# A low pass that contracts 64 rows, and one shared buffer for the low parts of two query sets

## The chip, the cores and the metric

The kernel runs on one core of one Trainium2 chip. The metric is the device time of one execution in microseconds (us); the time of a kernel is the median of its runs. The core's engines are named as the profile names them: PE is TensorE's matmul, PEld its weight load, DVE is VectorE, ACT is ScalarE, POOL is GpSimd and SP is SyncE, which issues most transfers.

## The reference

One decoder layer over 2048 tokens of width 1024, all in float32. An input projection feeds two head groups. Group A, which the change touches, is sparse attention with 8 query heads of 64 over 2 shared key heads. An indexer scores every key for every query, the 256 best causal keys are kept, and softmax attention runs over them:

```python
rel = jax.nn.relu(jnp.einsum('bthd,bsd->btsh', qib, ki))      # index scores, 8 heads x 64
iscore = jnp.einsum('btsh,bth->bts', rel, wib)
_, idx = lax.top_k(iscore, topk)                              # topk = 256
s = jnp.einsum('btgrd,btkgd->btgrk', qg, ksel) * (HEAD_DIM ** -0.5)
p = jax.nn.softmax(s, axis=-1)
o = jnp.einsum('btgrk,btkgd->btgrd', p, vsel)
```

Group B is a gated linear recurrence (HGRN2). Both groups' outputs pass an output projection, a norm and a residual, then a SwiGLU layer of width 2816 with its own norms and residual.

## The kernel before

The program has two phases. The first (`project_hgrn_phase`, up to some 890 us) makes the input projection and the recurrence. The second, `mixer_phase`, has the attention of 16 blocks of 128 queries, and lays the output projection and the SwiGLU layer between the attention's steps: `fills` gives each attention step ("slot") its share of these items by a table of weights, so that PE always has dense matmuls between two attention steps. All engines walk through the same slots, each in its own fixed order, and meet by semaphores.

Matmuls use the type fp32r, which keeps only a high part of a float32. So each operand is split: the high part is a copy that rounds, the low part is what remains. The dense products take three matmuls (high by high, high by low, low by high). The attention has head dimension 64, half of PE's 128 rows, and uses the other half for the split of the keys. The tile `KT` holds for each of three key sets (two key heads, one index key set, number `KV`) the high part on partitions 0 to 63 and the low part on 64 to 127. The queries `qT` and the index queries `qiT` have two planes: plane 0 has the high part of the queries on both halves of the partitions, plane 1 the low part on both halves. `two_passes` then needs two matmuls of 128 rows for queries by keys: plane 0 by `KT` is high by (high and low), plane 1 by `KT` is low by (high and low).

Per block the pieces of this are made as follows. `open_split` (PE, L1980) transposes 64 columns of the projected rows into the PSUM tile `SA`, eight times for queries, three times for keys. `high` (ACT) copies out the high part: keys in one instruction of 64x384 (L1524), queries in two of 64x1024, one for each half of the partitions (L1528, L1529). `low` (DVE) subtracts high from `SA` and gives the low part: keys straight to partitions 64 to 127 (L1696), queries to partitions 0 to 63 of plane 1 (L1704). `double` (ACT, L1538) copies that plane to partitions 64 to 127 and tells PE by the semaphores `q_doubled` and `qi_doubled`. `openings` says when: the queries of block b+1 at the last head of block b, the index queries and keys of block b+2 one head earlier. That makes 16 sets of queries and 14 of index queries, which blocks 0 and 1 don't need.

PE waits for `doubled` twice per block: before the index scores of block b+1 (`idx`) and before the scores of block b (`scores`). The index scores are read by ACT (L1546) and summed by DVE (L1716); the scores are read by DVE (L1810), go through the exponential on ACT (L1562), are transposed by PE (L2011), copied by ACT (L1574) and multiplied with the values by PE (L2025). `SA` has two halves that all of these take in turn.

Of the kernel before, what the change touches and what calls it, by code (L numbers as in the profile page):

```python
# [29 lines left out]
HEADS, KV, HD = 8, 2, 64  # L30
GROUP = HEADS // KV
ATT = HEADS * HD
IH = 8
# [16 lines left out]
SM_SCALE = HD ** -0.5  # L50
# [795 lines left out]
def mixer_phase(nc, a, proj_d, mix_d, x1_d, out, kept):  # L846
# [28 lines left out]
    for s in range(NS):  # L875
# [12 lines left out]
        for g, (f0, f1) in enumerate(GROUPS):  # L888
            last = f1 - 1 if g == NG - 1 else f1
# [95 lines left out]

    for b in range(NB):
        for c in range(pairs_of(b + 1) if 2 <= b + 1 < NB else 0):
            w = min(1024, NK(b + 1) - 1024 * c) / 1024
# [14 lines left out]
    for s in range(-1, NS - 1):  # L1003
# [3 lines left out]
        last = at["out", s + 1, 0, 0, 0] - 1  # L1007
        if s < 0:
            window = window[PARTS_FROM:]
            last = FIRST - 1  # L1010
# [13 lines left out]
    with ExitStack() as ctx:  # L1024
        def sb(name, shape, dt=F32):
            return ctx.enter_context(nc.sbuf_tensor(name, shape, dt))
# [10 lines left out]
        def sem(name):  # L1037
            return ctx.enter_context(nc.semaphore("m_" + name))
# [2 lines left out]
        wis = sb("wis", [P, 2, IH])  # L1041
        KT, acc_last = sb_two("KT", [P, 3, T], "acc_last", [P, 6, D])
        V = sb("V", [P, NB, KV * HD])
        qT = sb("qT", [P, 2, HEADS, P], F32R)
        qiT = sb("qiT", [P, 2, IH, P], F32R)
        score = sb("score", [P, T + 8])
        bias = sb("bias", [P, 2, T], BF16)
        ends = sb("ends", [P, 2])
# [45 lines left out]
        iota_ready = sem("iota_ready")  # L1094
        rows_ready, value0_ready = sem("rows_ready"), sem("value0_ready")
        hi_out = sem("hi_out")
        doubled = {"q": sem("q_doubled"), "qi": sem("qi_doubled")}
        sa_full = sem("sa_full")
        sa_free_act, sa_free_dve, pt_ready = sem("sa_free_act"), sem("sa_free_dve"), sem("pt_ready")
        rel_read = sem("rel_read")  # L1100
# [27 lines left out]
        use, reader, pt_order, idx_order, hi_order = {}, [], {}, {}, {}  # L1128
# [46 lines left out]
        def pair(key):  # L1175
            return SA[:, use[key] % 2, :]
# [3 lines left out]
        for key in use:  # L1180
            who = reader[use[key]]
            if who == "pt":
                _, b, h, p = key
# [7 lines left out]
        def wait_pair_read(eng, n):  # L1191
            eng.wait_ge(*pair_read[n])
# [5 lines left out]
        def wait_pair_full(eng, key):  # L1198
            eng.wait_ge(sa_full, use[key] + 1)
# [42 lines left out]
        def heads(ap, n):  # L1242
            return ap.rearrange("p (h t) -> p h t", h=n)
# [272 lines left out]
        def _(act):  # L1516
            s_ = nc.scalar

            def high(key):

                what, b = key
                wait_pair_full(act, key)
                if what == "keys":
                    s_.activation(KT[0:HD, :, b * P:(b + 1) * P], heads(pair(key)[0:HD, 0:3 * P], 3), ACT.Copy)\  # L1524
                      .then_inc(hi_out, 1)
                else:
                    to, scale = (qT, -SM_SCALE) if what == "q" else (qiT, 1.0)
                    s_.activation(to[HD:P, 0], heads(pair(key)[0:HD], 8), ACT.Copy, scale=scale)  # L1528
                    s_.activation(to[0:HD, 0], heads(pair(key)[0:HD], 8), ACT.Copy, scale=scale)\  # L1529
                      .then_inc(hi_out, 1)  # L1530

            def double(b, h):

                for key in openings(b, h):
                    if key[0] != "keys":
                        to = qT if key[0] == "q" else qiT
                        wait_pair_read(act, use[key])
                        s_.activation(to[HD:P, 1], to[0:HD, 1].bitcast(F32), ACT.Copy).then_inc(doubled[key[0]], 1)  # L1538

            def idx(b, c, h):  # L1540
                w = min(1024, NK(b) - 1024 * c)
# [106 lines left out]

            for key in openings(-1, 0):
                high(key)  # L1650
            double(-1, 0)
            for b in range(NB):
                for c in range(pairs_of(b + 1) if 2 <= b + 1 < NB else 0):
                    for h in range(IH):
                        idx(b + 1, c, h)
                        fill(("i", b, c, h))
                softmax(b, 0)
                fill(("s", b))
                for h in range(HEADS):
                    for key in openings(b, h):  # L1660
                        high(key)
                        if key[0] == "qi":
                            fill(("O", b, 0))
                    fill(("A", b, h))
                    turned_probs(b, h, 0)
                    fill(("B", b, h))
                    if h + 1 < HEADS:
                        softmax(b, h + 1)
                    if pairs_of(b) == 2:
                        turned_probs(b, h, 1)  # L1670
                        fill(("C", b, h))
                    for k in search(b, h, "B"):
                        count(b + 1, k)
                    double(b, h)
            for n in range(TAIL[0], LAST_STEP):
                step(n)

# [2 lines left out]
        def _(dve):  # L1680
            v = nc.vector
# [8 lines left out]
            def low(key):  # L1690

                what, b = key
                dve.wait_ge(hi_out, hi_order[key] + 1)
                if what == "keys":
                    cols = slice(b * P, (b + 1) * P)
                    v.tensor_tensor(KT[HD:P, :, cols], heads(pair(key)[0:HD, 0:3 * P], 3),  # L1696
                                    KT[0:HD, :, cols].bitcast(F32), ALU.subtract).then_inc(sa_free_dve, 1)
                else:
                    to = (qT if what == "q" else qiT)[0:HD]
                    if what == "q" and b >= 1:  # L1700
                        dve.wait_ge(doubled["q"], b)
                    if what == "qi" and b >= 3:
                        dve.wait_ge(doubled["qi"], b - 2)
                    v.scalar_tensor_tensor(to[:, 1], heads(pair(key)[0:HD], 8), -SM_SCALE if what == "q" else 1.0,  # L1704
                                           to[:, 0].bitcast(F32), ALU.mult, ALU.subtract).then_inc(sa_free_dve, 1)

            def accumulate(b, c, h):
                w = min(1024, NK(b) - 1024 * c)
# [253 lines left out]
        def _(pe):  # L1962
            t = nc.tensor
# [16 lines left out]
                    last = t.transpose(pair(key)[0:HD, h * P:(h + 1) * P], row[:, b % 2, c0:c0 + HD], ident[:])  # L1980
                last.then_inc(sa_full, 1)

            def two_passes(to, q, k):
                t.matmul(to, q[:, 0], k, start=True, stop=False)  # L1984
                return t.matmul(to, q[:, 1], k, start=False, stop=True)  # L1985

            def idx(b, c, h):
                key = ("idx", b, c, h)
                take(key)
                for k0 in range(1024 * c, min(NK(b), 1024 * (c + 1)), 512):  # L1990
                    w = min(512, NK(b) - k0)
                    last = two_passes(pair(key)[:, k0 - 1024 * c:k0 - 1024 * c + w], qiT[:, :, h, :], KT[:, KV, k0:k0 + w])
                last.then_inc(sa_full, 1)

            def scores(b, h):
                for p in range(pairs_of(b)):
                    key = ("att", b, h, p)
                    take(key)
                    for k0 in range(1024 * p, min(NK(b), 1024 * (p + 1)), 512):
                        w = min(512, NK(b) - k0)  # L2000
                        last = two_passes(pair(key)[:, k0 - 1024 * p:k0 - 1024 * p + w], qT[:, :, h, :],
                                          KT[:, h // GROUP, k0:k0 + w])
                    last.then_inc(sa_full, 1)

            def turn_probs(b, h, p):
# [99 lines left out]
            for b in range(NB):  # L2105
                if 2 <= b + 1 < NB:
                    wait_pair_read(pe, use["keys", b + 1])
                    pe.wait_ge(doubled["qi"], b)
                    for c in range(pairs_of(b + 1)):
                        for h in range(IH):  # L2110
                            idx(b + 1, c, h)
                            fill(("i", b, c, h))
                wait_pair_read(pe, use["keys", b])
                pe.wait_ge(doubled["q"], b + 1)
                scores(b, 0)
                fill(("s", b))
                for h in range(HEADS):
                    if h + 1 < HEADS:
                        scores(b, h + 1)
                    for key in openings(b, h):  # L2120
                        open_split(key)
                        if key[0] == "qi":
                            fill(("O", b, 0))
                    fill(("A", b, h))
                    for p in range(pairs_of(b)):
                        turn_probs(b, h, p)
                        fill(("BC"[p], b, h))
                        values(b, h, p)
# [51 lines left out]
```

## Time and profile before

| | us |
|---|---|
| median of 3 runs | 3378.53 |
| lowest, highest run | 3377.57, 3380.3 |
| the profiled execution | 3383.49 |
| its span, first to last instruction | 3381.5 |

| engine | busy us | share |
|---|---|---|
| PE | 3214.6 | 95% |
| PEld | 2836.7 | 84% |
| DVE | 2267.9 | 67% |
| ACT | 1501.5 | 44% |
| POOL | 237.1 | 7% |

Starts and durations in the rows are from one profiled execution. A row of the timeline gives the start, the duration, the engine and line, the tiles written and read, and in brackets how long the engine was idle before it and what ended that. Matmuls are pipelined: the next one starts before the end of the last, so the distance from start to start is what one costs, not its duration. The last column of a waiting engine's row names what came last by the profile.

### The profile page before, as it was taken

How to read it: one execution, taken by the hardware profiler on the slowest of the kernel's cores; microseconds unless marked ns; L12 is line 12 of the kernel's file. 1: busy time of each engine (PE TensorE's matmuls, PEld its weight loads, DVE VectorE, ACT ScalarE, POOL GpSimd, SP SyncE). 2: the span in 40 equal slices, each digit the busy share in tenths (PEclk: the TensorE clock that was granted, in tenths of full speed). 3: DMA queues.
4: the chain of work that ended last, by engine and by line, in shares of the span. 5: the costliest groups of instructions: out<-in, count | busy, mean ns of one | idle time of the engine just before them, and what ended most of it. 6: DMA issues, size and time to landing. Idle time of an engine off the chain costs nothing.

```text
span 3381.5 us, 46512 instructions
## 1 busy us (share of the span) xinstructions
PE 3214.6 (95%) x18048; PEld 2836.7 (84%) x18048; DVE 2267.9 (67%) x3817; ACT 1501.5 (44%) x2477; POOL 237.1 (7%) x400
## 2 busy tenths in 40 slices
PE   8999999999888899999989999998999999989998
PEld 8999999998777788888778888887888888868886
DVE  3467777788565766666787777677876765463445
ACT  3454455445455454443554444445554444333222
POOL 0000000000111110010110001011000000010000
PEclk9999999999899999999989999999999999999999
DMA  5543443344222222222522212134111112252233
GB/s 182 168 134 121 131 149 125 114 139 130 98 84 104 94 83 80 68 85 69 180 83 76 71 63 79 64 111 150 63 65 60 64 52 74 95 182 97 91 105 107
DMA packets 147501, 345.66 MB, mean 102 GB/s; under 512 B 15057, under 2 KB 35921, under 8 KB 145233
## 3 DMA queue, kind: packets, MB, share of 16 engines
q1 hardware_dynamic: 144976, 338.49, 30.2%
q10 hardware_dynamic: 2304, 4.20, 0.3%
q8 instruction: 144, 2.36, 0.3%
q14 instruction: 77, 0.62, 0.1%
HBM read 283.31 MB, written 59.31 MB: 101 GB/s over the span
## 4 chain that ended last, share of the span: by engine, by line
PE 63%; DVE 5%; ACT 2%; issue 2%; DMA 1%; SPq 0%; DVEq 0%; POOL 0%; ACTq 0%; POOLq 0%
PE PJ_d L2069 9%; PE PJ_d L2071 9%; PE PJ_d L2070 9%; PE SC L2025 7%; PE PJ_d L2094 6%; PE PJ_d L2096 6%; PE PJ_d L2095 6%; PE SA L1984 3%; PE SA L2011 3%; PE SA L1985 3%; PE SA L1980 1%; DVE score L1716 1%; DVE wd_lo L1825 1%; DVE prob L1810 1%; DVE h_lo L1830 0%
## 5 line engine op out<-in xcount | busy, mean ns | idle before, releaser
L2069 PE MATMUL PJ_d<-h_hi,wd_hi 128*128 128x512 f32 (+1 forms) x1472 | 577.1, 392 | 15.4 <-DVE h_lo L1830 9.9
L2071 PE MATMUL PJ_d<-h_hi,wd_lo 128*128 128x512 f32 (+1 forms) x1472 | 564.6, 384 | 0.0
L2070 PE MATMUL PJ_d<-h_lo,wd_hi 128*128 128x512 f32 (+1 forms) x1472 | 563.8, 383 | 0.0
L1579 ACT ACTIVATE wd_hi<-wd_raw 128x512 fp32r<-128x512 f32 x568 | 345.2, 627 | 229.6 <-DMA wd_raw<-in_w_gu 128.6
L733 PE MATMUL PJ<-w_hi,h_hi 128*128 128x338 f32 (+1 forms) x1280 | 416.0, 325 | 2.8 <-DVE w_lo L550 2.8
L1825 DVE TENSOR_TENSOR wd_lo<-wd_raw,wd_hi 128x512 fp32r<-128x512 f32 x568 | 380.5, 689 | 45.9 <-ACT wd_hi L1579 42.9
L734 PE MATMUL PJ<-w_lo,h_hi 128*128 128x338 f32 (+1 forms) x1280 | 408.6, 319 | 0.0
L735 PE MATMUL PJ<-w_hi,h_lo 128*128 128x338 f32 (+1 forms) x1280 | 408.5, 319 | 0.0
L1574 ACT ACTIVATE pT<-SA 128x512 f32<-128x512 f32 (+3 forms) x320 | 156.6, 532 | 519.4 <-PE SA L2011 519.4
L1810 DVE CUSTOM_DVE_ANT_0 prob<-SA,bias 128x1024 f32<-128x1024 f32 (+7 forms) x192 | 170.1, 911 | 314.2 <-PE SA L1985 306.9
L2069 PEld LDWEIGHTS PJ_d<-h_hi,wd_hi 128*128 128x128 f32 x1472 | 280.8, 191 | 66.4 <-DVE wd_lo L1825 6.8
L2071 PEld LDWEIGHTS PJ_d<-h_hi,wd_lo 128*128 128x128 f32 x1472 | 280.4, 190 | 54.8
L2070 PEld LDWEIGHTS PJ_d<-h_lo,wd_hi 128*128 128x128 f32 x1472 | 281.2, 191 | 48.7
L2025 PEld LDWEIGHTS SC<-V,pT 128*128 128x128 f32 x2176 | 273.9, 194 | 38.1 <-ACT pT L1574 26.6
L2025 PE MATMUL SC<-V,pT 128*128 128x64 f32 x2176 | 271.1, 274 | 19.8 <-ACT pT L1574 19.8
L2094 PE MATMUL PJ_d<-wd_hi,hid 128*128 128x512 f32 x704 | 282.0, 401 | 6.9 <-DVE acc L1864 3.6
L2096 PE MATMUL PJ_d<-wd_hi,hid 128*128 128x512 f32 x704 | 276.1, 392 | 0.0
L2095 PE MATMUL PJ_d<-wd_lo,hid 128*128 128x512 f32 x704 | 275.6, 391 | 0.0
L428 ACT ACTIVATE stage<-PJ 128x338 f32<-128x338 f32 (+1 forms) x160 | 72.7, 454 | 430.6 <-PE PJ L735 430.6
L733 PEld LDWEIGHTS PJ<-w_hi,h_hi 128*128 128x128 f32 x1280 | 242.5, 189 | 5.4 <-issue 3.1
L734 PEld LDWEIGHTS PJ<-w_lo,h_hi 128*128 128x128 f32 x1280 | 243.0, 190 | 2.3
L735 PEld LDWEIGHTS PJ<-w_hi,h_lo 128*128 128x128 f32 x1280 | 242.1, 189 | 0.0
(207 smaller groups left out, 5724.6 us busy)
## 6 DMA issues: line engine op xcount, KB each, us to landing
wd_raw<-in_w_gu SPq DMA_DIRECT2D x352, 256.0 KB, 2.9
wd_raw<-in_w_down SPq DMA_DIRECT2D x176, 256.0 KB, 2.6
w_raw<-in_w_in SPq DMA_DIRECT2D x40, 684.0 KB, 4.6
w_raw<-in_w_in SPq DMA_DIRECT2D x40, 676.0 KB, 4.5
row_h<-proj_d SPq DMA_DIRECT2D x16, 1024.0 KB, 7.0
proj_d<-stage SPq DMA_DIRECT2D x40, 342.0 KB, 4.5
proj_d<-stage SPq DMA_DIRECT2D x40, 338.0 KB, 5.0
x_d<-acc SPq DMA_DIRECT2D x24, 512.0 KB, 2.9
```

Source lines behind the costliest of these rows:

```text
L733: t.matmul(out, h_hi[:, k, tok], w_hi[:, u, e], start=(k == 0), stop=False)
L734: t.matmul(out, h_hi[:, k, tok], w_lo[:, u, e], start=False, stop=False)
L735: last = t.matmul(out, h_lo[:, k, tok], w_hi[:, u, e], start=False, stop=(k == KD - 1))
L1579: s_.activation(w_hi[:, u % RING, :], w_raw[:, u % RING, :], ACT.Copy).then_inc(w_hi_ready, 1)
L1825: v.tensor_tensor(w_lo[:, u % RING, :], w_raw[:, u % RING, :], w_hi[:, u % RING, :].bitcast(F32), ALU.subtract).then_inc(w_lo_ready, 1)
L2025: last = t.matmul(SC[:, h * HD:(h + 1) * HD], pT[:, m % 2, (kb % 4) * P:(kb % 4 + 1) * P], V[:, kb, g * HD:(g + 1) * HD], start=(kb == 0), ...
L2069: t.matmul(to[:, tok], w_hi[:, r, w], h_hi[:, c, tok], start=(c == 0 and part != 1), stop=False)
L2070: t.matmul(to[:, tok], w_hi[:, r, w], h_lo[:, c, tok], start=False, stop=False)
L2071: last = t.matmul(to[:, tok], w_lo[:, r, w], h_hi[:, c, tok], start=False, stop=(c == KD - 1 and part != 0))
L2094: t.matmul(to, hi, w_hi[:, r, :], start=(k == parts[0]), stop=False)
L2095: t.matmul(to, hi, w_lo[:, r, :], start=False, stop=False)
L2096: last = t.matmul(to, lo, w_hi[:, r, :], start=False, stop=(k == parts[-1]))
```

## The change

The high parts stay as they were, on both halves of the partitions, but `qT` and `qiT` lose their second plane. A new tile `qlow` holds both low parts: that of the queries on partitions 0 to 63, that of the index queries on 64 to 127. The second matmul of `two_passes` contracts only the 64 rows on which the low part lies, with the high part of the keys. For the index keys that needs the high part on partitions 64 to 127, so the index set of `KT` is stored with its halves exchanged, and the copy and the subtraction of the keys become two instructions each on ACT and DVE. `double` and its semaphores go; PE waits for DVE's low part itself. The product of the low part of the queries with the low part of the keys is no longer in the sum.

```diff
-        qT = sb("qT", [P, 2, HEADS, P], F32R)
-        qiT = sb("qiT", [P, 2, IH, P], F32R)
+        qT = sb("qT", [P, HEADS, P], F32R)
+        qiT = sb("qiT", [P, IH, P], F32R)
+        qlow = sb("qlow", [P, HEADS, P], F32R)
...
                 if what == "keys":
-                    s_.activation(KT[0:HD, :, b * P:(b + 1) * P], heads(pair(key)[0:HD, 0:3 * P], 3), ACT.Copy)\
-                      .then_inc(hi_out, 1)
+                    cols = slice(b * P, (b + 1) * P)
+                    s_.activation(KT[0:HD, 0:KV, cols], heads(pair(key)[0:HD, 0:KV * P], KV), ACT.Copy)
+                    s_.activation(KT[HD:P, KV, cols], pair(key)[0:HD, KV * P:(KV + 1) * P], ACT.Copy).then_inc(hi_out, 1)
...
-            def double(b, h):
-
-                for key in openings(b, h):
-                    if key[0] != "keys":
-                        to = qT if key[0] == "q" else qiT
-                        wait_pair_read(act, use[key])
-                        s_.activation(to[HD:P, 1], to[0:HD, 1].bitcast(F32), ACT.Copy).then_inc(doubled[key[0]], 1)
...
                 if what == "keys":
                     cols = slice(b * P, (b + 1) * P)
-                    v.tensor_tensor(KT[HD:P, :, cols], heads(pair(key)[0:HD, 0:3 * P], 3),
-                                    KT[0:HD, :, cols].bitcast(F32), ALU.subtract).then_inc(sa_free_dve, 1)
+                    v.tensor_tensor(KT[HD:P, 0:KV, cols], heads(pair(key)[0:HD, 0:KV * P], KV),
+                                    KT[0:HD, 0:KV, cols].bitcast(F32), ALU.subtract)
+                    v.tensor_tensor(KT[0:HD, KV, cols], pair(key)[0:HD, KV * P:(KV + 1) * P],
+                                    KT[HD:P, KV, cols].bitcast(F32), ALU.subtract).then_inc(sa_free_dve, 1)
+                elif what == "q":
+                    v.scalar_tensor_tensor(qlow[0:HD], heads(pair(key)[0:HD], 8), -SM_SCALE, qT[0:HD].bitcast(F32),
+                                           ALU.mult, ALU.subtract).then_inc(sa_free_dve, 1)
                 else:
...
+                    v.tensor_tensor(qlow[HD:P], heads(pair(key)[0:HD], 8), qiT[HD:P].bitcast(F32),
+                                    ALU.subtract).then_inc(sa_free_dve, 1)
...
-            def two_passes(to, q, k):
-                t.matmul(to, q[:, 0], k, start=True, stop=False)
-                return t.matmul(to, q[:, 1], k, start=False, stop=True)
+            def two_passes(to, high, k, low, k_high):
+                t.matmul(to, high, k, start=True, stop=False)
+                return t.matmul(to, low, k_high, start=False, stop=True)
...
-                    last = two_passes(pair(key)[:, k0 - 1024 * c:k0 - 1024 * c + w], qiT[:, :, h, :], KT[:, KV, k0:k0 + w])
+                    last = two_passes(pair(key)[:, k0 - 1024 * c:k0 - 1024 * c + w], qiT[:, h, :], KT[:, KV, k0:k0 + w],
+                                      qlow[HD:P, h, :], KT[HD:P, KV, k0:k0 + w])
...
-                        last = two_passes(pair(key)[:, k0 - 1024 * p:k0 - 1024 * p + w], qT[:, :, h, :],
-                                          KT[:, h // GROUP, k0:k0 + w])
+                        last = two_passes(pair(key)[:, k0 - 1024 * p:k0 - 1024 * p + w], qT[:, h, :],
+                                          KT[:, h // GROUP, k0:k0 + w], qlow[0:HD, h, :], KT[0:HD, h // GROUP, k0:k0 + w])
...
-                    pe.wait_ge(doubled["qi"], b)
+                    wait_pair_read(pe, use["qi", b + 1])
...
-                pe.wait_ge(doubled["q"], b + 1)
+                wait_pair_read(pe, use["q", b])
```

On ACT, around the end of block 0's attention, this stood in a row before: the openings of index queries (L1528, L1529), keys (L1524) and queries, each set of queries followed by its copy (L1538), and then the index scores of block 2 (L1546).

```order
534 L1529 ACTIVATE qiT<-SA 64x1024
535 L1606 ACTIVATE acc<-PJ_d 128x512
536 L1579 ACTIVATE wd_hi<-wd_raw_9646 128x512
537 L1524 ACTIVATE KT<-SA 64x3x128
538 L1574 ACTIVATE pT<-SA 128x128
539 L1562 ACTIVATE prob,den<-prob,nmx 128x128
540 L1538 ACTIVATE qiT<-qiT 64x1024
541 L1528 ACTIVATE qT<-SA 64x1024
542 L1529 ACTIVATE qT<-SA 64x1024
543 L1606 ACTIVATE acc<-PJ_d 128x512
544 L1574 ACTIVATE pT<-SA 128x128
545 L1538 ACTIVATE qT<-qT 64x1024
546 L1546 ACTIVATE prob<-SA 128x384 x3
```

In the changed kernel, with its own line numbers (the keys are L1525 and L1526, the queries L1529 and L1530, the index scores L1539), the same place reads:

```order
535 L1530 ACTIVATE qiT<-SA 64x1024
536 L1599 ACTIVATE acc<-PJ_d 128x512
537 L1572 ACTIVATE wd_hi<-wd_raw_9646 128x512
538 L1525 ACTIVATE KT<-SA 64x2x128
539 L1526 ACTIVATE KT<-SA 64x128
540 L1567 ACTIVATE pT<-SA 128x128
541 L1555 ACTIVATE prob,den<-prob,nmx 128x128
542 L1529 ACTIVATE qT<-SA 64x1024
543 L1530 ACTIVATE qT<-SA 64x1024
544 L1599 ACTIVATE acc<-PJ_d 128x512
545 L1567 ACTIVATE pT<-SA 128x128
546 L1539 ACTIVATE prob<-SA 128x384 x3
```

Both copies are gone, the keys have two instructions, and nothing else has moved. On PE, at the start of the second phase (11 transposes, then the scores of the first two heads), the rows before were:

```order
4390 L1980 MATMUL SA<-ident,xt 64x128 x11
4391 L1984 MATMUL SA<-KT,qT 128x128
4392 L1985 MATMUL SA<-KT,qT 128x128
4393 L1984 MATMUL SA<-KT,qT 128x128
4394 L1985 MATMUL SA<-KT,qT 128x128
4395 L2036 MATMUL PJ_d<-ident,tile_9647 128x128 x4
```

and now they are:

```order
4390 L1971 MATMUL SA<-ident,xt 64x128 x11
4391 L1975 MATMUL SA<-KT,qT 128x128
4392 L1976 MATMUL SA<-KT,qlow 128x128
4393 L1975 MATMUL SA<-KT,qT 128x128
4394 L1976 MATMUL SA<-KT,qlow 128x128
4395 L2028 MATMUL PJ_d<-ident,tile_9647 128x128 x4
```

PE has as many matmuls in the same order, with as many columns; every second one of a pair now reads 64 rows of `qlow` and `KT`.

## Rows read from the trace of the kernel before

**Rows 1.** The page: busy time, share of the span, instructions of each engine.

```profile
PE 3214.6 (95%) x18048; PEld 2836.7 (84%) x18048; DVE 2267.9 (67%) x3817; ACT 1501.5 (44%) x2477; POOL 237.1 (7%) x400
```

**Rows 2.** Stages: stretch, length; busy of PE, PEld, DVE, ACT, POOL; granted clock; DMA share.

```profile
890.00:1110.00 220.00, 184.37 (x958) 150.14 (x958) 124.65 (x338) 119.04 (x241) 38.14 (x90) 0.92 0.29 104
...
2600.00:2940.00 340.00, 336.81 (x1868) 290.20 (x1867) 210.75 (x341) 141.85 (x220) 4.48 (x2) 1.00 0.22 73
```

**Rows 3.** Line 1985, the low pass: count, min/median/max ns, first and last start.

```profile
L1985 PE MATMUL SA<-KT,qT x320: 272/390/628, 898.8 to 2932.9; 128*128 128x512 f32 x136, 128*128 128x128 f32 x8, 128*128 128x256 f32 x8, 128*128 128x384 f32 x8
...
L1985 PE MATMUL SA<-KT,qiT x304: 272/390/628, 931.9 to 2665.0; 128*128 128x512 f32 x136, 128*128 128x384 f32 x8, 128*128 128x128 f32 x4, 128*128 128x256 f32 x4
```

**Rows 4.** Timeline of PE: values of one head, then scores of the next.

```profile
2043.80 0.78 PE L2025 MATMUL SC<-V,pT 128*128 128x64 f32 x6
2044.39 0.48 PE L1984 MATMUL SA<-KT,qT 128*128 128x512 f32 x1
2044.70 0.39 PE L1985 MATMUL SA<-KT,qT 128*128 128x512 f32 x1
2044.93 0.40 PE L1984 MATMUL SA<-KT,qT 128*128 128x512 f32 x1
2045.16 0.40 PE L1985 MATMUL SA<-KT,qT 128*128 128x512 f32 x1
```

**Rows 5.** Timeline of PE: three transposes with a tile of 128*64 between dense matmuls.

```profile
1185.94 0.39 PE L2071 MATMUL PJ_d<-h_hi,wd_lo 128*128 128x512 f32 x1
1186.17 0.49 PE L1980 MATMUL SA<-ident,xt 128*64 128x128 f32 x3
1186.42 0.48 PE L2069 MATMUL PJ_d<-h_hi,wd_hi 128*128 128x512 f32 x1
1186.73 0.39 PE L2070 MATMUL PJ_d<-h_lo,wd_hi 128*128 128x512 f32 x1
```

**Rows 6.** Timeline of PE: three transposes with the full tile, then dense matmuls.

```profile
2040.71 0.50 PE L2011 MATMUL SA<-ident,prob 128*128 128x128 f32 x3
2040.96 0.48 PE L2094 MATMUL PJ_d<-wd_hi,hid 128*128 128x512 f32 x1
2041.28 0.39 PE L2095 MATMUL PJ_d<-wd_lo,hid 128*128 128x512 f32 x1
```

**Rows 7.** Timeline of all engines at the start of the second phase.

```profile
896.10 1.22 DVE L1704 SCALAR_TENSOR_TENSOR qT<-SA,qT 64x1024 fp32r<-64x1024 f32 x1 [1.81 <-ACT qT L1529]
...
897.35 1.05 ACT L1538 ACTIVATE qT<-qT 64x1024 fp32r<-64x1024 f32 x1 [1.28 <-DVE qT L1704]
...
898.51 0.45 PE L1984 MATMUL SA<-KT,qT 128*128 128x128 f32 x1 [4.52 <-ACT qT L1538]
...
901.01 1.11 PE L2036 MATMUL PJ_d<-ident,tile 128*128 128x128 f32 x4 [1.42 <-DMA tile<-mix_d]
```

**Rows 8.** Waits of PE from 914 to 1110 us: total us, times, longest.

```profile
PE SC L2025 <- ACT pT L1574: 10.6, 17, 2.0
...
PE SA L1984 <- ACT prob L1546: 4.1, 9, 1.9
```

**Rows 9.** Timeline at the end of block 0: the copy, the index scores, PE.

```profile
931.50 1.06 ACT L1538 ACTIVATE qT<-qT 64x1024 fp32r<-64x1024 f32 x1 [0.19 <-DVE qT L1704]
...
932.58 0.87 ACT L1546 ACTIVATE prob<-SA 128x384 f32<-128x384 f32 x2
...
933.12 0.44 PE L1984 MATMUL SA<-KT,qiT 128*128 128x384 f32 x1 [0.57 <-ACT prob L1546]
```

**Rows 10.** Timeline at a late copy: what PE has meanwhile.

```profile
1467.55 1.67 PE L2025 MATMUL SC<-V,pT 128*128 128x64 f32 x14
```

**Rows 11.** By line: the copy, the keys on ACT, the keys on DVE (min/median/max ns).

```profile
L1538 ACT ACTIVATE qT<-qT x16: 1054/1058/1064, 897.4 to 2810.1; 64x1024 fp32r<-64x1024 f32 x16
...
L1524 ACT ACTIVATE KT<-SA x16: 471/485/488, 893.2 to 2592.5; 64x384 fp32r<-64x384 f32 x16
...
L1696 DVE TENSOR_TENSOR KT<-SA,KT x16: 550/551/552, 893.7 to 2593.4; 64x384 fp32r<-64x384 f32 x16
```

More of the change, by code:

```diff
@@ L1096, in mixer_phase @@
         hi_out = sem("hi_out")
-        doubled = {"q": sem("q_doubled"), "qi": sem("qi_doubled")}
         sa_full = sem("sa_full")
@@ L1523, in high @@
                 if what == "keys":
-                    s_.activation(KT[0:HD, :, b * P:(b + 1) * P], heads(pair(key)[0:HD, 0:3 * P], 3), ACT.Copy)\
-                      .then_inc(hi_out, 1)
+                    cols = slice(b * P, (b + 1) * P)
+                    s_.activation(KT[0:HD, 0:KV, cols], heads(pair(key)[0:HD, 0:KV * P], KV), ACT.Copy)
+                    s_.activation(KT[HD:P, KV, cols], pair(key)[0:HD, KV * P:(KV + 1) * P], ACT.Copy).then_inc(hi_out, 1)
                 else:
                     to, scale = (qT, -SM_SCALE) if what == "q" else (qiT, 1.0)
-                    s_.activation(to[HD:P, 0], heads(pair(key)[0:HD], 8), ACT.Copy, scale=scale)
-                    s_.activation(to[0:HD, 0], heads(pair(key)[0:HD], 8), ACT.Copy, scale=scale)\
+                    s_.activation(to[HD:P], heads(pair(key)[0:HD], 8), ACT.Copy, scale=scale)
+                    s_.activation(to[0:HD], heads(pair(key)[0:HD], 8), ACT.Copy, scale=scale)\
                       .then_inc(hi_out, 1)
-            def double(b, h):
-                for key in openings(b, h):
-                    if key[0] != "keys":
-                        to = qT if key[0] == "q" else qiT
-                        wait_pair_read(act, use[key])
-                        s_.activation(to[HD:P, 1], to[0:HD, 1].bitcast(F32), ACT.Copy).then_inc(doubled[key[0]], 1)
             def idx(b, c, h):
@@ L1650, in _ @@
                 high(key)
-            double(-1, 0)
             for b in range(NB):
@@ L1673, in _ @@
                         count(b + 1, k)
-                    double(b, h)
             for n in range(TAIL[0], LAST_STEP):
@@ L1695, in low @@
                     cols = slice(b * P, (b + 1) * P)
-                    v.tensor_tensor(KT[HD:P, :, cols], heads(pair(key)[0:HD, 0:3 * P], 3),
-                                    KT[0:HD, :, cols].bitcast(F32), ALU.subtract).then_inc(sa_free_dve, 1)
-                else:
[L1699 to L1705, printed above, removed]
+                    v.tensor_tensor(KT[HD:P, 0:KV, cols], heads(pair(key)[0:HD, 0:KV * P], KV),
[5 more added lines that the diff above has]
+                                           ALU.mult, ALU.subtract).then_inc(sa_free_dve, 1)
+                else:
+                    v.tensor_tensor(qlow[HD:P], heads(pair(key)[0:HD], 8), qiT[HD:P].bitcast(F32),
+                                    ALU.subtract).then_inc(sa_free_dve, 1)
             def accumulate(b, c, h):
```

## The prediction

> **What bounds the kernel now.** I read the busy times first: PE is busy for 95% of the span, ACT for 44%, DVE for 67% [rows 1]. Then the stages: in the stretch in which the second phase starts PE is idle for 220 - 184.4 = 35.6 us, in a late one with long rows of keys for only 340 - 336.8 = 3.2 us [rows 2]. So from about the third block on the end of the kernel is set by the number of matmuls and by their distance from start to start, and only the first 220 us of the phase have idle time that lighter work on another engine could give back. Third, the passes that the change touches: the low pass runs 320 times for scores and 304 times for index scores, 624 in all, up to 512 columns each, and most of the phase long [rows 3]. From start to start one such matmul takes 0.23 us (2044.70 to 2044.93 to 2045.16), while its duration reads 0.39 to 0.40 [rows 4]: each starts 0.16 to 0.17 us before the end of the last. The dense matmuls have the same distance.
>
> **Part 1, the copy on ACT goes.** It is 16 copies of queries and 14 of index queries, 1.06 us each [rows 11], 31.7 us of ACT. ACT isn't the bound, so it counts only where PE waits for ACT just behind a copy.
>
> The clearest place is the start of the phase: PE waits 4.52 us, and the copy ends that wait at 898.4 [rows 7]. Without it PE would start when DVE's low part is ready, at 896.10 + 1.22 = 897.3, so about 1.1 us sooner. But look at what is late next: after four small matmuls PE waits again, at 901.01, for the transfer of `tile` from `mix_d` [rows 7]. That transfer neither waits for the copy nor for PE, so it lands when it did, and the 1.1 us are added to the 1.42 us of that wait. I book nothing here.
>
> The second kind of place is the end of a block: at 931.50 ACT makes the copy, at 932.58 it turns to the index scores, and PE waits 0.57 us for them at 933.12 [rows 9]. Without the copy ACT starts when PE's second pair is full, some 0.3 us sooner. All waits of PE on the two ACT steps that can stand behind a copy, in the stretch 914 to 1110, come to 10.6 + 4.1 = 14.7 us in 26 waits [rows 8], and most of these stand elsewhere in the blocks. Behind the eight copies there I take 1.5 us, at the rate of 0.3 us for those with a wait behind them; the bounds are 0 and 1.06 x 8 = 8.5 us. In late blocks the copy is covered: while ACT copies at 1466.4, PE has dense matmuls and then 1.67 us of values that are long ready [rows 10]. Term: -1.5 us, from 0 to -8.5.
>
> **Part 2, the keys in two instructions.** On ACT 384 columns take 0.485 us [rows 11] and 1024 take 1.06, so a column costs (1.058 - 0.485) / 640 = 0.9 ns and an instruction by itself 0.485 - 0.344 = 0.14 us. On DVE, 0.551 for 384 [rows 11] and 1.22 for 1024 [rows 7] give 0.15 us. So the keys of a block are ready, and their half of `SA` is free, 0.3 us later, 16 times: 4.7 us if nothing covered it. What covers it is the dense work of the slot between the opening and the next use of that half, as for the copy. Who waits is PE's next transposes, and only in the first blocks. At the start of the phase the extra 0.14 us on ACT lies in the wait for the transposes of the queries and in the slack before the transfer. Term: +0.3 us, from 0 to 4.7. The low part of the index queries is one DVE instruction of the same size with inputs and output on other partitions; the old keys' subtraction already crossed from partitions 0 to 63 to 64 to 127, at a rate no worse than the queries': nothing.
>
> **Part 3, the low pass has 64 rows.** It has the same number of columns, and PE's time goes by columns, so the pass itself has no reason to be shorter. At the clock's upper level of 2.4 GHz 512 columns are 0.213 us, so the distance of 0.23 leaves at most 0.017 x 624 = 10.6 us to be gained if smaller loads or passes closed up, and I see no row that says they would. The open question is what it costs to go from a matmul of 128 rows to one of 64 and back, 2 x 624 = 1248 times, since every low pass stands between full ones. No row of this trace has a 64-row tile. The nearest is the other kind of partial tile: the transposes L1980 use 128*64, 64 columns of the array. They start 0.23 us after the dense matmul ahead of them, last (1186.42 - 1186.17) = 0.25 us for three, and the dense matmuls behind follow after 0.31 [rows 5]. Three transposes with the full tile take 0.25 us as well, and the dense ones behind them follow after 0.32 [rows 6]. So going to a tile of half the columns and back costs less than 0.01 us. The upper end comes from the overlap of 0.16 us [rows 4]: if each matmul had to end before one of another tile starts, 1248 x 0.16 = 200 us. In between lies what happens when a pair follows the plain float32 products of the values: the first matmul reads 0.48 instead of 0.39 and its successor starts after 0.31 instead of 0.23, an exposed 0.08 to 0.09 us [rows 4]; once per low pass that would be 624 x 0.08 = 50 us, in both directions 100. I take zero, because the partial tile is nearest in kind, and keep 0 to 200 for the range. Term: 0.
>
> **The rule that speaks against it.** The rows of the transposes show no stop on the way to a half tile or back [rows 5, 6]. The Trainium skill, "TensorEngine Tiling (Array Packing)", section Key Properties, says that changing the tiling mode, not just the tile, drains TensorE. By this rule the sum would have the full overlap lost at every change, +200 us; by the rows, nothing. The trace disagrees for a tile of half the columns; for one of half the rows no row here shows it, and so the rule stays as a rival.
>
> **Sum.** -1.5 + 0.3 + 0 = -1.2 us. Against the profiled execution of 3383.5 us that gives 3382.3. That execution was 5.0 us above the median of 3378.5; taken from the median, the forecast is 3377.3.
>
> **The rivals.** *A stop at the change of tile, in part* (slower). The mechanism is in the pairs of the score passes: the 64-row load or matmul can't be taken up while a 128-row one is under way, so part of the overlap is lost. It decides at very little: 6.8 us / 1248 = 5.4 ns per change are enough to be measured. At 0.01 to 0.05 us per change it gives 12 to 62 us, 3390 to 3440. For it: PE has no slack to swallow it in the late stages [rows 2], and nothing here has shown such a tile. Against it: rows 5 and 6.
>
> *A stop of the full overlap* (slower by much): 3378 + 100 to 200 = 3478 to 3578, by the mechanism worked out in part 3. The skill's rule on tiling modes, named above, would make it so.
>
> *ACT's relief reaches the path, or the passes close up* (faster). Up to 8.5 us behind the early copies, up to 10.6 us from shorter distances: 3360 to 3371. For it: PE does wait on ACT in the early stretch [rows 8]. Against it: most waits there aren't behind a copy, and what is saved is met by the next wait, as at 901.01 [rows 7].
>
> *The change lets the granted clock fall.* It is 0.92 in the early stretch and 1.00 in a late one [rows 2]. If passes of half the rows made the array look idler, score-heavy stretches could drop to 1.2 GHz; that would cost 0.23 us per matmul while it lasts, and it ends in the range of the first rival. I count it there.
>
> **How the numbers follow.** Forecast case, no cost per change and a relief near 1 us: 0.50, with its own range 3371 to 3385. Partial stop: 0.26. Full stop: 0.13. Faster: 0.11. About 0.2%, 6.8 us, is what a measurement of this kernel can tell from no change. From the forecast case I give 0.02 to faster and 0.04 to slower, for the way in which small shifts move the waits. Faster: 0.11 + 0.02 = 0.13. Same: 0.44. Slower: 0.26 + 0.13 + 0.04 = 0.43. The likeliest case gives the time. The range leaves out most of the full stop and the outer end of the faster case: 3367 to 3438.
>
> **What would show it.** In the profile after: the low pass should start 0.23 us after the high pass and the next matmul 0.23 us after it; 0.3 or more there is the stop. A full stop would read as 0.39. The row of L1538 should be gone, ACT busy down by about 29 us, and PE at the start of the phase should begin at about 897.4 and still wait for the transfer until 901.0. The waits on the index scores at a block's end should shrink, not vanish. I would be wrong if PE's idle time in the early stretch fell by more than 8 us, or if PE's busy time rose.

## The result and the profile after

| kernel | median us | lowest to highest | ratio to before |
|---|---|---|---|
| before | 3379.3 (4 runs) | 3377.6 to 3380.3 | |
| changed | 3604.3 (4 runs) | 3597.2 to 3608.6 | 1.066 (95% interval 1.065 to 1.067) |

The change costs 225 us. The forecast was 3377.3 with a range up to 3438, so the time lies outside the range and on the other side. Even the rival of a full stop (3478 to 3578) falls short of it. The profiled execution of the changed kernel took 3597.2 us, 213.7 more than that of before; the reading below is made between these two. The other three runs of the changed kernel took 3604.0 to 3608.6 us.

The page of the changed kernel, first its span and the busy times of the engines (share of the span, instructions), beside which [rows 1] stand:

```profile
span 3595.4 us, 46493 instructions
...
PE 3456.7 (96%) x18048; PEld 2848.9 (79%) x18048; DVE 2277.8 (63%) x3833; ACT 1477.8 (41%) x2463; POOL 226.6 (6%) x400
```

PE has as many instructions and is busy 3456.7 - 3214.6 = 242.1 us longer. The span grows by 213.9 us, so PE's idle time has fallen by 28.2 us: what PE lost took the place of waits it had anyway. ACT is busy 23.7 us less, from the copies, and that shows nowhere.

The line of the low pass, with its tile, count and min/median/max ns, and what its load was idle for, beside [rows 3]:

```profile
L1976 PEld LDWEIGHTS SA<-KT,qlow x624: 182/183/285, 900.2 to 3147.5; 64*128 64x128 f32 x156
L1976 PE MATMUL SA<-KT,qlow x624: 322/492/542, 900.2 to 3147.5; 64*128 64x512 f32 x136, 64*128 64x384 f32 x8, 64*128 64x128 f32 x6, 64*128 64x256 f32 x6
its engine sat idle before it (us, times) until:
  issue: 133.6, 518
```

The median of a low pass has gone from 390 to 492 ns, and its weight load, idle for 8.9 + 9.7 = 18.6 us in all before (scores and index scores), is idle for 133.6 us in 518 pieces. "Issue" means that no semaphore is the reason. The timeline shows how, for PE and its load (the answer to [rows 4], now with the load's rows):

```profile
2416.40 0.40 PE L2088 MATMUL PJ_d<-wd_hi,hid 128*128 128x512 f32 x1
2416.40 0.19 PEld L1975 LDWEIGHTS SA<-KT,qiT 128*128 128x128 f32 x1
...
2416.63 0.39 PE L1975 MATMUL SA<-KT,qiT 128*128 128x512 f32 x1
2416.95 0.18 PEld L1976 LDWEIGHTS SA<-KT,qlow 64*128 64x128 f32 x1 [0.36 <-issue]
2416.95 0.49 PE L1976 MATMUL SA<-KT,qlow 64*128 64x512 f32 x1
2417.37 0.19 PEld L1975 LDWEIGHTS SA<-KT,qiT 128*128 128x128 f32 x1 [0.24 <-issue]
2417.37 0.49 PE L1975 MATMUL SA<-KT,qiT 128*128 128x512 f32 x1
2417.80 0.18 PEld L1976 LDWEIGHTS SA<-KT,qlow 64*128 64x128 f32 x1 [0.24 <-issue]
2417.80 0.50 PE L1976 MATMUL SA<-KT,qlow 64*128 64x512 f32 x1
```

Take the first two loads. The load of L1975 has the tile of the matmul ahead of it, 128*128; it starts at 2416.40, with that matmul, and is over before its own matmul starts at 2416.63, 0.23 later. The load of L1976 has the tile 64*128. It doesn't start at 2416.63 with the matmul ahead of it, but at 2416.95, in the same moment as its own matmul. So two things are lost. The columns of the matmul of 2416.63 take 512 / 2.4 GHz = 0.213 us, to 2416.84, and the load waits 0.10 to 0.11 us longer (of which 0.017 is in every step), as I read it until the array has run empty. Then the pass has to wait for its load, so its duration reads 0.49 instead of 0.39, and whatever follows is late by another 0.10. From 2416.95 on, where every matmul has another tile than the last, both are paid at each step: 0.42 to 0.43 us instead of 0.23, about 0.196 us per change, into the low pass as well as out of it. 1248 x 0.196 = 245 us, beside 242.1 us by which PE's busy time grew (0.194 per change).

The granted clock has only a small part in it. It was 0.983 in the profiled execution before and 0.982 in the one after; the share that was missing, times the span, is 0.017 x 3381.5 = 57 us before and 0.018 x 3595.4 = 65 us after, so up to some 8 us by this estimate. In the other three runs of the changed kernel it was 0.977, and they took 7 to 11 us longer. So a part of the 225 us between the medians is the clock's.

### The profile page after: what moved, and what is told of

It is laid out like the page before. It is cut to its first block, busy times and chain, and to the rows that moved or that the text cites. A ratio compares the mean times of both kernels' runs of the same rounds, so it can differ in the third digit from the quotient of the medians.

```text
span 3595.4 us, 46493 instructions
## 1 busy us (share of the span) xinstructions
PE 3456.7 (96%) x18048; PEld 2848.9 (79%) x18048; DVE 2277.8 (63%) x3833; ACT 1477.8 (41%) x2463; POOL 226.6 (6%) x400
## 4 chain that ended last, share of the span: by engine, by line
PE 68%; DVE 4%; ACT 1%; issue 1%; DMA 1%; SPq 0%; DVEq 0%; POOL 0%; ACTq 0%; POOLq 0%
PE PJ_d L2061 9%; PE PJ_d L2063 9%; PE PJ_d L2062 9%; PE SA L1976 6%; PE PJ_d L2086 6%; PE SC L2017 6%; PE PJ_d L2087 6%; PE PJ_d L2088 6%; PE SA L1975 6%; PE SA L2003 3%; PE SA L1971 1%; DVE prob L1801 0%; DVE wd_lo L1816 0%; DVE h_lo L1821 0%; ACT h_hi L1585 0%
## 5 line engine op out<-in xcount | busy, mean ns | idle before, releaser
L2061 PE MATMUL PJ_d<-h_hi,wd_hi 128*128 128x512 f32 (+1 forms) x1472 | 588.9, 400 | 15.6 <-DVE h_lo L1821 10.0
L1976 PE MATMUL SA<-KT,qlow 64*128 64x512 f32 (+3 forms) x624 | 291.2, 467 | 0.0
L1539 ACT ACTIVATE prob<-SA 128x1024 f32<-128x1024 f32 (+7 forms) x176 | 143.8, 818 | 321.7 <-PE SA L1976 310.8
L1707 DVE SCALAR_TENSOR_TENSOR score<-prob,wis,score 128x1024 f32<-128x1024 f32 (+7 forms) x154 | 158.3, 1028 | 172.8 <-ACT prob L1539 170.4
```

Source lines behind the costliest of these rows:

```text
L1976: return t.matmul(to, low, k_high, start=False, stop=True)
L2061: t.matmul(to[:, tok], w_hi[:, r, w], h_hi[:, c, tok], start=(c == 0 and part != 1), stop=False)
```

## The experiments

The theory (A) is that the time is lost at each change of the tile's height, and nowhere else. The rivals: (B) it is the place of the operands, the shared buffer or the new waits; (C) a pass of 64 rows is slow by itself. Beside them two terms of the sum were open: what the copy on ACT was worth, and what the split keys cost.

### Everything but the 64 rows

```diff
-                                      qlow[HD:P, h, :], KT[HD:P, KV, k0:k0 + w])
+                                      qlow[:, h, :], KT[:, KV, k0:k0 + w])
...
-                                          KT[:, h // GROUP, k0:k0 + w], qlow[0:HD, h, :], KT[0:HD, h // GROUP, k0:k0 + w])
+                                          KT[:, h // GROUP, k0:k0 + w], qlow[:, h, :], KT[:, h // GROUP, k0:k0 + w])
...
                     wait_pair_read(pe, use["qi", b + 1])
+                    wait_pair_read(pe, use["q", b])
```

The upper half of `qlow` is also set to zero once at the start.

> Everything of the change (shared buffer, no copy, keys in two instructions) but the low pass contracts all 128 rows of qlow and KT, so that the other set's low part is summed in as well; PE waits for both low parts ahead of the index scores. Theory A (the time is lost at each change between 128 and 64 rows): all of the loss goes, the time is within 3 us of before, 3376 to 3382, and the low pass starts 0.23 us after the high one. Rival B (the loss comes from where the operands lie or from the waits that replaced the semaphores of the copy): the time stays near 3600.

Measured: 3380.5 us, ratio 1.000 (0.999 to 1.001). The low pass has its old duration, and no stop is listed ahead of its load:

```profile
L1978 PEld LDWEIGHTS SA<-KT,qlow x624: 187/188/338, 900.7 to 2931.7; 128*128 128x128 f32 x156
L1978 PE MATMUL SA<-KT,qlow x624: 272/390/632, 900.8 to 2932.0; 128*128 128x512 f32 x136, 128*128 128x384 f32 x8, 128*128 128x128 f32 x6, 128*128 128x256 f32 x6
```

The whole loss goes with the height of the tile: its median of 3380.5 us stands beside 3380.4 of the kernel before. B falls: the buffer, the exchanged halves of `KT`, the waits are all in this kernel.

### Only the 64 rows

```diff
-                return t.matmul(to, q[:, 1], k, start=False, stop=True)
+                return t.matmul(to, q[0:HD, 1], k[0:HD], start=False, stop=True)
```

> The kernel before with one edit: the second pass contracts rows 0 to 63 of both operands, for scores and index scores; copy, buffers, keys as before. Theory A: the whole loss is here, 3600 to 3610, steps of 0.42 to 0.43 us into and out of the low pass. Rival B: at most half of it, under 3490.

Measured: 3599.9 us, ratio 1.065 (1.063 to 1.066), PE busy 3458.1 us; A's range began 0.1 us above that. The one edit makes the whole loss, with all passes on partitions 0 to 63. The first experiment takes the loss away and this one makes it, so the mechanism is in the second matmul's rows. It doesn't yet tell a slow pass from a dear change.

### The same passes, fewer changes

```diff
-            def two_passes(to, high, k, low, k_high):
-                t.matmul(to, high, k, start=True, stop=False)
-                return t.matmul(to, low, k_high, start=False, stop=True)
+            def two_passes(made):
+                for to, high, k, low, k_high in made:
+                    t.matmul(to, high, k, start=True, stop=False)
+                for to, high, k, low, k_high in made:
+                    last = t.matmul(to, low, k_high, start=False, stop=True)
+                return last
```

`idx` and `scores` collect the chunks of a unit in `made` and call it once.

> The changed kernel, but in each unit of up to 1024 keys the high passes of all its chunks go first and the low ones behind them: 736 changes between 128 and 64 rows in place of 1248, as many passes. Theory A (0.20 us per change): 512 x 0.196 = 100 us less than the changed kernel, 3500 to 3515, and 0.23 us from the first low pass to the second. Rival C (a pass of 64 rows is itself slow, 0.4 us longer than one of 128): no difference, 3600 to 3608.

Measured: 3489.0 us, ratio 1.032 (1.030 to 1.033): 115 us less than the changed kernel, where A said 100 and C nothing. The time came out under A's range of 3500 to 3515. Between the two profiled executions it is 3595.4 - 3485.9 = 109.5 us, and up to 9 us of that is the granted clock by the estimate above (0.984 here, 0.982 there: 0.016 x 3485.9 = 56 us missing beside 65); the changed kernel's median run had only 0.977. The columns of the passes don't explain the surplus, since the price is nearly the same for a narrow chunk. These are passes of 128 columns in the changed kernel:

```profile
1048.01 0.33 PE L1975 MATMUL SA<-KT,qiT 128*128 128x128 f32 x1
1048.26 0.32 PE L1976 MATMUL SA<-KT,qlow 64*128 64x128 f32 x1
1048.52 0.50 PE L2086 MATMUL PJ_d<-wd_hi,h_hi 128*128 128x512 f32 x1
```

and in the kernel before:

```profile
1033.75 0.22 PE L1984 MATMUL SA<-KT,qiT 128*128 128x128 f32 x1
1033.81 0.28 PE L1985 MATMUL SA<-KT,qiT 128*128 128x128 f32 x1
1033.92 0.45 PE L2094 MATMUL PJ_d<-wd_hi,h_hi 128*128 128x512 f32 x1
```

The step into the low pass takes 0.25 us instead of 0.06, so 0.19 more, and the one out of it 0.26 instead of 0.11. One unit of two chunks of the grouped kernel in the timeline of PE and its load (rows marked x2 hold two instructions):

```profile
2447.61 0.30 PEld L1976 LDWEIGHTS SA<-KT,qT 128*128 128x128 f32 x2
2447.64 0.71 PE L1976 MATMUL SA<-KT,qT 128*128 128x512 f32 x2
2448.28 0.29 PEld L1978 LDWEIGHTS SA<-KT,qlow 64*128 64x128 f32 x2 [0.36 <-issue]
2448.28 0.73 PE L1978 MATMUL SA<-KT,qlow 64*128 64x512 f32 x2
2448.94 0.30 PEld L1976 LDWEIGHTS SA<-KT,qT 128*128 128x128 f32 x2 [0.37 <-issue]
```

The loads stop once per pair of passes, not once per pass. The second load of each pair follows the first at once, beside the running pass. A's other figure missed: it said 0.23 us from the first low pass to the second. The two low passes with the step behind them take 2448.94 - 2448.28 = 0.66 us, some 0.34 for the first step and 0.32 for the second, because the first low pass of the pair still has its late load behind it. The rows settle one more thing: the low pass behind the change writes the first chunk's part of `SA`, the high pass ahead of it the second's, and the stop is there all the same. So it doesn't hang on both passes of a pair adding into the same place.

### More passes, as many changes

```diff
                 t.matmul(to, high, k, start=True, stop=False)
+                t.matmul(to, low, k_high, start=False, stop=False)
+                t.matmul(to, low, k_high, start=False, stop=False)
                 return t.matmul(to, low, k_high, start=False, stop=True)
```

> The changed kernel with the low pass issued three times in a row in place of once (so the low part is summed in three times): 1248 more passes of 64 rows, but as many changes of tile height. Theory A (only the change costs): a further 64-row pass costs what a 128-row one does, 0.23 us at 512 columns, in all 275,456 columns x 2 / 2.4 GHz + 1248 x 0.015 = 248 us: 3830 to 3855, and 0.23 us from the second low pass to the third. Rival C (each pass of 64 rows is slow, 0.43): more than 4050.

Measured: 3877.8 us, 273.5 us above the changed kernel, or 0.219 us for each of the 1248 further passes. C asked for more than 4050 and falls. The sum of A was some 25 us too low, and the time lies above its range of 3830 to 3855. The timeline, with the three low passes as L1976, L1977 and L1978:

```profile
2411.30 0.18 PEld L1976 LDWEIGHTS SA<-KT,qlow 64*128 64x128 f32 x1 [0.25 <-issue]
2411.30 0.50 PE L1976 MATMUL SA<-KT,qlow 64*128 64x512 f32 x1
2411.41 0.19 PEld L1977 LDWEIGHTS SA<-KT,qlow 64*128 64x128 f32 x1
2411.64 0.39 PE L1977 MATMUL SA<-KT,qlow 64*128 64x512 f32 x1
2411.64 0.18 PEld L1978 LDWEIGHTS SA<-KT,qlow 64*128 64x128 f32 x1
...
2411.87 0.39 PE L1978 MATMUL SA<-KT,qlow 64*128 64x512 f32 x1
2412.19 0.19 PEld L1975 LDWEIGHTS SA<-KT,qT 128*128 128x128 f32 x1 [0.36 <-issue]
2412.19 0.50 PE L1975 MATMUL SA<-KT,qT 128*128 128x512 f32 x1
```

From the second low pass to the third it is 0.23 us, exactly what a 128-row pass takes. From the first to the second it is 0.34: that is the late load of the first. From the third to the full tile it is 0.32: the array running empty, 0.09 to 0.10. So a 64-row pass isn't slow, and the two halves of the price stand apart here. A's sum counted every column at the clock's upper level, and the granted clock was 0.971 here against 0.982 in the changed kernel's profiled execution: 0.029 x 3874.6 = 112 us missing beside 65, so up to 47 us by the estimate above, where these two executions are 279.2 - 248 = 31 us further apart than the sum. So the clock can cover what the sum missed; no run holds it fixed to show that it does.

### Other rows, same height

```diff
-                for to, high, k, low, k_high in made:
-                    last = t.matmul(to, low, k_high, start=False, stop=True)
+                for n, (to, high, k, low, k_high) in enumerate(made):
+                    half = slice(n % 2 * HD, n % 2 * HD + HD)
+                    last = t.matmul(to, low[half], k_high[half], start=False, stop=True)
```

This starts from the grouped kernel, with the whole of `qlow` and `KT` handed to `two_passes`.

> The grouped kernel, but the second low pass of a unit reads partitions 64 to 127 instead of the rows of the first (for scores it takes the index queries' low part and the other way about, so its sum is another one; PE waits for both low parts). Tile height stays 64 between the two low passes, only the rows change; both write different banks. If only a change of height costs: as grouped, 3482 to 3491, 0.34 us from one low pass to the next. If a change of rows costs as much: 256 x 0.2 = 51 us more, 3540. If the two halves of the rows run at the same time: up to 256 x 0.2 us less, 3435 to 3460, and far below 0.23 us between the starts.

Measured: 3446.9 us, ratio 1.020 (1.018 to 1.022): 42 us less than the grouped kernel. The same place in its timeline:

```profile
2458.24 0.71 PE L1978 MATMUL SA<-KT,qT 128*128 128x512 f32 x2
2458.88 0.19 PEld L1981 LDWEIGHTS SA<-KT,qlow 64*128 64x128 f32 x2 [0.36 <-issue]
2458.88 0.50 PE L1981 MATMUL SA<-KT,qlow 64*128 64x512 f32 x2
...
2459.31 0.30 PEld L1978 LDWEIGHTS SA<-KT,qT 128*128 128x128 f32 x2 [0.24 <-issue]
2459.31 0.56 PE L1978 MATMUL SA<-KT,qT 128*128 128x512 f32 x2
```

Both loads together take 0.19 us, the time of one, and both passes together 0.50, the time of one; in the grouped kernel two passes took 0.73. So going from rows 0 to 63 to rows 64 to 127 costs nothing, and the two halves of the array work at the same time when they write different banks. The full-height passes on either side still pay for the change, and the kernel stays 68 us behind the one of before.

### The index scores alone

```diff
+            def two_passes(to, q, k, rows=slice(0, P)):
...
+                return t.matmul(to, q[rows, 1], k[rows], start=False, stop=True)
...
+                                      slice(0, HD))
```

The last line is the argument in `idx`; the rest is the kernel before.

> The kernel before with 64 rows in the low pass of the index scores alone (304 of 624 passes, 608 of 1248 changes). If the price is per change wherever it stands: 608 / 1248 of the 220 us that all of them cost, 3480 to 3495. If the scores, where DVE and ACT wait for PE, carry it: under 3440.

Measured: 3484.8 us, ratio 1.031 (1.029 to 1.033): 105.4 us over before, or 0.173 us per change, beside 219.5 / 1248 = 0.176 for all passes. The scores were not run alone; by the difference they have (219.5 - 105.4) / 640 = 0.178. So the price is the same at the index scores, which ACT reads, as at the scores, which DVE reads. It is PE's own time, not somebody's wait.

### The copy on ACT alone

`double` and its semaphores go, as in the change; plane 1 of `qT` and `qiT` stays, with zeros on partitions 64 to 127, written once on DVE:

```diff
+            link(v.tensor_copy(qT[HD:P, 1], heads(score[HD:P, 0:1024], 8)))
...
+            link(v.tensor_copy(qiT[HD:P, 1], heads(score[HD:P, 0:1024], 8)))
```

> The kernel before without the copy: plane 1 holds the low part on partitions 0 to 63 and zeros, written once, on 64 to 127; both passes contract 128 rows. It leaves out the product of both low parts, as the changed kernel does. Prices the relief of ACT alone: 31.7 us of ACT gone, my sum said 1.5 us, 3377 to 3379; the rival that ACT's relief reaches the path says 3368 to 3372.

Measured: 3375.9 us, ratio 0.9987 (0.9978 to 0.9996), between the two ranges named. A second time, beside the split keys:

> The version without the copy, as before in e4, beside the split one on the same chip. If the relief of ACT is real, 3374 to 3378 and again under the kernel before by 0.1%; if the first run was chance, 3379 to 3381.

Measured: 3377.6 us, ratio 0.9995 (0.9987 to 1.0004). So the relief of ACT is worth 2.5 to 4.5 us by the medians, and only the first of the two intervals leaves out zero. The place where it was looked for shows it: between 914 and 1110 us PE waited 4.1 us in 9 waits for the index scores on ACT before [rows 8], and here 2.9 us in 8 and 1.8 us in 7. That is 1.2 to 2.3 us; what the medians have beyond it stands in no wait that was found. The start of the phase behaves as read from [rows 7]; this is the timeline of PE in the first of these runs:

```profile
897.29 0.44 PE L1972 MATMUL SA<-KT,qT 128*128 128x128 f32 x1 [3.43 <-DVE qT L1691]
...
900.99 1.11 PE L2024 MATMUL PJ_d<-ident,tile 128*128 128x128 f32 x4 [2.62 <-DMA tile<-mix_d]
```

PE starts its scores 1.2 us sooner, at 897.29 instead of 898.51, waits 2.62 us for the transfer instead of 1.42, and goes on at 900.99 instead of 901.01. In the second run the whole phase began 2.4 us later, and of the wait for the transfer 1.77 us were left.

### The keys in two instructions

The zeros version plus the split on both engines, with all three sets laid out as before:

```diff
-                    s_.activation(KT[0:HD, :, b * P:(b + 1) * P], heads(pair(key)[0:HD, 0:3 * P], 3), ACT.Copy)\
-                      .then_inc(hi_out, 1)
+                    cols = slice(b * P, (b + 1) * P)
+                    s_.activation(KT[0:HD, 0:KV, cols], heads(pair(key)[0:HD, 0:KV * P], KV), ACT.Copy)
+                    s_.activation(KT[0:HD, KV, cols], pair(key)[0:HD, KV * P:(KV + 1) * P], ACT.Copy).then_inc(hi_out, 1)
```

> The version without the copy and with zeros, plus the keys in two instructions on ACT and on DVE (all three sets laid out as before). My sum gave the split 0.3 us, bounds 0 and 4.7: 3376 to 3377. If the split is what sets the full-rows version, which came to 3380.5, apart from the zeros version at 3375.9, it is 3379 to 3381.

Measured: 3378.7 us, ratio 0.9996 (0.9987 to 1.0005), 2.9 us above the unsplit version and between the two ranges named. But the two were not measured on one chip, and 2.9 us is the size of the spread, so both were measured again on the same one:

> The same with the keys in two instructions. If the split costs 3 us (e8 beside e4), it comes out 2 to 4 us above e10_zeros_again; by my sum 0.3 us above it, which can't be told from nothing.

Measured: 3378.1 us, ratio 0.9995 (0.9986 to 1.0004), 0.5 us above e10_zeros_again. The 2.9 us didn't come back; the split isn't told from nothing.

## Why the prediction was wrong

**The bound was read rightly.** PE sets the end ([rows 1, 2]), and a few nanoseconds per change were enough to be seen, as the first rival said: nearly all of the 225 us came from 1248 changes, with no other engine taking part.

**Part 3, the low pass, is the step that failed.** "I take zero, because the partial tile is nearest in kind." The transposes with 128*64 do change the tile without a stop [rows 5, 6], and they do so in the changed kernel too (0.23 us from the dense matmul of 927.55 to them). (The way out is the weaker witness: behind transposes of either tile the load of the next dense matmul starts only 0.03 us before it, at 1186.39 for 1186.42 in [rows 5], so a late load couldn't be told apart there.) But their tile is as high as the array, and a half tile in columns says nothing on one in rows. The count of 1248 and the reason for the pass itself not being dearer both held: 0.23 us between two 64-row passes. What was mis-sized is the price of a change: 0 in the sum, 0.19 to 0.20 us measured, or 1248 x 0.196 = 245 us, of which 28 went into waits that PE had anyway.

**The upper bound was too low as well.** I took 0.16 us, the end of one matmul over the start of the next [rows 4], and called 200 us the full stop. That counts the running empty, but not that a load which can't go ahead has to be made in the open before its pass can start. The trace of before had the second half of the price: the 0.08 to 0.09 us behind the values [rows 4] is a pass whose load came late. It stands in the same trace, just ahead of the pass of 2044.39:

```profile
2044.36 0.19 PEld L1984 LDWEIGHTS SA<-KT,qT 128*128 128x128 f32 x1
2044.39 0.48 PE L1984 MATMUL SA<-KT,qT 128*128 128x512 f32 x1
```

I used it as a price in its own right, somewhere between the ends, when it had to be added to the other. Measured from the moment the columns are through (0.213 us), the array is empty for 0.10 to 0.11, and the load shows for 0.10; less the 0.017 of every step that is the price.

**The rule of the Trainium skill.** What decided was the rule I had weighed against the rows: "TensorEngine Tiling (Array Packing)", section Key Properties, says that changing the tiling mode, not just the tile, drains TensorE. For the height of a tile the runs agree: a change between 128 rows and 64 costs 0.19 to 0.20 us each way, one from the lower to the upper 64 rows nothing. For 128*64 among 128*128 the trace disagrees, less than 0.01 us. I gave the rule 0.13 because a neighbouring row contradicted it; the row was of another dimension, and the rule should have had the larger part.

**Part 1, the copy.** -1.5 us was forecast, bounds 0 to -8.5; the two runs alone gave -4.5 and -2.5, and the waits on the index scores shrank by 1.2 and 2.3 us. The version with 128 rows, which has this term and the next, stands 0.1 us above the kernel before, where the sum said 1.2 us less; the spread of the runs is larger than either. The reading of the start was right to 0.1 us in the first of these runs: nothing is won there, since the transfer is late next. In the changed kernel the phase began 2.3 us later: PE's wait fell from 4.52 to 3.43 us as forecast, but it began at 899.84 and not at 897.4.

**Part 2, the keys.** +0.3 us was forecast and can't be told from nothing (0.5 us and 2.9 us in two pairs of runs).

**The signs named for a stop.** "A full stop would read as 0.39" for the step was short of 0.42 to 0.43 for the reason above. The row of the copy is gone, ACT's busy time is 23.7 us lower (forecast some 29), and PE's busy time rose, which I had named as a sign of being wrong. The other such sign came too: in the stretch 890 to 1110 PE was idle for 220 - 195.7 = 24.3 us instead of 35.6, so 11.3 us less, where I had named 8; the longer steps fill its waits, and the waits on the index scores are gone from there. The rival that the granted clock falls is not the cause: the grouped kernel has as many passes of 64 rows, a clock of 0.984, and still takes 109 us more than before. But the clock was a little lower in the changed kernel (0.982 and 0.977), and whether half rows bring that about was not shown.

**The range.** It left out the whole of the second rival, 3478 to 3578, and not most of it, as the text beside it says; part 3 had kept 0 to 200 us for the range, which then ended some 60 us above the kernel before. With a term that could be 0 or 200 us by a mechanism that one row speaks for and one rule against, a range up to 3438 was a choice for the row.

## What to carry to other kernels

A matmul that contracts 64 rows among ones of 128 is not cheaper and pays about 0.2 us each time the tile's height changes, so where an operand fills only half the rows, put zeros on the other half and keep the full height; that also did away with the copy here, at 3376 to 3378 us. If 64-row tiles are wanted, put them in a row and on both halves with different banks, where two run in the time of one; even so the kernel here stayed 68 us behind, since full-height passes stood on either side. And before a row of the trace is taken as the price of something it doesn't show, ask along which dimension the two agree.

## What the runs showed of the hardware

- A change of the tile's height between 128 and 64 rows costs 0.19 to 0.20 us each way at 512 columns: some 0.10 us in which the array runs empty, and 0.10 us for a weight load that starts only with its own matmul. At 128 columns the step into the low pass grew by as much, from 0.06 to 0.25 us. That the array runs empty is read from the times, not shown by a counter. Whether a load of fewer columns shortens the second part was not measured.
- Matmuls of 64 rows on the same rows follow each other in 0.23 us at 512 columns, as those of 128 rows do.
- Two matmuls of 64 rows on different halves, into different banks, ran at the same time: two in 0.50 us, their loads together in 0.19.
- A tile of 128*64 among tiles of 128*128 costs nothing that could be seen.
